# Seven small edits to a two-layer decoder trunk in fp32 on one core: unrolled MLP turns, split loads and weight tiles, an earlier spill, a changed order in the gated attention stage and at the end

## The reference, cut to what matters

```python
for layer in range(DEPTH):
    h = rmsnorm(x, norm_mix[layer])
    if layer % 2 == 0:
        m, ... = even_mixer(h, ...)   # retention and RG-LRU behind one projection
    else:
        m, gs = odd_mixer(h, ...)     # gated linear attention (GLA) by chunks
    x = x + m
    h = rmsnorm(x, norm_mlp[layer])
    x = x + jnp.square(jax.nn.relu(h @ w_up[layer])) @ w_down[layer]
y = rmsnorm(x, norm_final)
```

## Time and profile before

| | |
|---|---|
| device time, median of 3 runs | 2491.69 us (2489.11 to 2498.32) |
| the profiled execution's own time | 2490.22 us |
| its span, first to last instruction | 2488.4 us |
| TensorE (PE) matmul busy | 2436.4 us, 98% |
| DVE, ACT, POOL busy | 58%, 31%, 42% |
| mean granted TensorE clock | 0.993 of full |

### The profile page before, as it was taken

One profiled execution on the slowest core, in us unless ns is written; L12 is line 12 of the kernel. 1 busy time (PEld: TensorE's weight loads), 2 busy tenths in 40 slices (PEclk: granted clock), 3 DMA queues, 4 the chain that ended last, 5 costly groups with the idle time before them and its releaser, 6 DMA issues. The chain is left out here.

```text
span 2488.4 us, 40883 instructions
## 1 busy us (share of the span) xinstructions
PE 2436.4 (98%) x15934; PEld 2386.6 (96%) x15934; DVE 1438.0 (58%) x2082; ACT 771.0 (31%) x1222; POOL 1044.1 (42%) x773
## 2 busy tenths in 40 slices
PE   8999999999999999999999999999999999999998
PEld 8999999999999999999889889899999999999997
DVE  6974356345545544566767776756445545545576
ACT  4711442223223222223233453441222222222233
POOL 2343224354565465474212112224354554564571
PEclk9999999999999999999989999999999999999999
DMA  4123031111111111113101111131111111111112
GB/s 148 35 62 95 19 125 43 43 52 43 52 43 43 52 52 43 43 52 115 61 18 62 43 45 45 52 117 51 43 43 43 52 43 52 52 43 43 52 51 81
DMA packets 40010, 140.08 MB, mean 56 GB/s; under 512 B 6209, under 2 KB 9921, under 8 KB 38561
## 3 DMA queue, kind: packets, MB, share of 16 engines
q1 hardware_dynamic: 32192, 104.55, 13.1%
q10 hardware_dynamic: 7648, 33.04, 3.6%
HBM read 120.46 MB, written 14.88 MB: 54 GB/s over the span
## 5 line engine op out<-in xcount | busy, mean ns | idle before, releaser
L702 PE MATMUL PS<-RB,WH 128*128 128x384 f32 (+1 forms) x4368 | 1085.3, 330 | 6.3 <-issue 6.3
L702 PEld LDWEIGHTS PS<-RB,WH 128*128 128x128 f32 x4368 | 770.7, 188 | 15.5 <-issue 12.5
L702 PE MATMUL PS<-RA,WH 128*128 128x272 f32 (+2 forms) x3520 | 771.1, 309 | 11.5 <-DVE RA L1787 10.3
L702 PE MATMUL PS<-RB,WL 128*128 128x384 f32 (+1 forms) x2232 | 730.1, 327 | 0.0
L619 POOL TENSOR_TENSOR WH<-WR,FEW 128x1024 fp32r<-128x1024 f32 x128 | 247.0, 1930 | 1118.3 <-PE PS L702 1093.7
L702 PEld LDWEIGHTS PS<-RA,WH 128*128 128x128 f32 x3520 | 588.6, 188 | 16.0 <-issue 11.7
L702 PE MATMUL PS<-RA,WL 128*128 128x272 f32 (+2 forms) x1760 | 541.5, 308 | 0.0
L702 PEld LDWEIGHTS PS<-RB,WL 128*128 128x128 f32 x2232 | 420.1, 188 | 0.0
L622 POOL TENSOR_TENSOR WL<-WR,WH 128x1024 fp32r<-128x1024 f32 x128 | 340.9, 2664 | 10.0
L702 PEld LDWEIGHTS PS<-RA,WL 128*128 128x128 f32 x1760 | 331.5, 188 | 0.0
L1886 DVE TENSOR_TENSOR X<-PS,X 128x544 f32<-128x544 f32 x280 | 202.5, 724 | 203.7 <-PE PS L702 203.7
(11 more groups left out here) (223 smaller groups left out, 2335.0 us busy)
## 6 DMA issues: line engine op xcount, KB each, us to landing
WR<-ws SPq DMA_DIRECT2D x189, 512.0 KB, 3.4
X<-xT ACTq DMA_DIRECT2D x8, 544.0 KB, 7.7
EB<-xT ACTq DMA_DIRECT2D x8, 544.0 KB, 5.5
x_spill<-X ACTq DMA_DIRECT2D x1, 4352.0 KB, 15.8
EB<-x_spill ACTq DMA_DIRECT2D x8, 544.0 KB, 7.0
GA<-st_gla ACTq DMA_DIRECT2D x4, 1024.0 KB, 5.3
glas_o<-GA ACTq DMA_DIRECT2D x4, 1024.0 KB, 5.0
yT<-X SPq DMA_DIRECT2D x16, 208.0 KB, 1.9
```

The costliest lines, as they stand in the source:

```text
L702: return nc.tensor.matmul(out, lhsT, rhs, start=start, stop=stop, skip_group_check=True)
```

## The change

Seven edits. (1) Start: ACT loads tiles 0 to 3 of X and SP tiles 4 to 7; ACT and DVE split the first weight tile, and the first tile of X in three column groups; TensorE runs 16 matmuls of ONES by ONES first. (2) `parts` works in QW = 4 pieces of 256 columns; all counts of `w_high` and `w_split` are four times as large. (3) TensorE's MLP loop is written out (the other engines keep theirs). (4) The spill is 8 DMAs, one after each tile's square. (5) Even order: one half group S ahead of the first RA; RH 4 and RH 5 after RCO 3; RES earlier. (6) GLA order: L after B instead of before, GN2 after the last Q of its turn. (7) End: the last square goes to TensorE directly, `last_log` and `last_exp` are apart, and OUT_AT scales the second group later.

```diff
@@ even_schedule
-    s.append(("RA", EORDER[0]))
+    s += take(1) + [("RA", EORDER[0])]
@@
-            s += take(2 if k < 2 else 1)
+            s += take(2 if k == 1 else 1)
@@
-            s += [("RCU", 0, 0), ("RCU", 0, 1), ("RN2", 1), ("RCU", 1, 0), ("RCU", 1, 1)] + take(1) + [("RH", 4), ("RCO", 2)]
-            s += [("RCU", 2, 0), ("RCU", 2, 1), ("RX", 3, 0), ("RX", 0, 1), ("RH", 5), ("RCO", 3), ("RHL", 4)]
+            s += [("RCU", 0, 0), ("RCU", 0, 1), ("RN2", 1), ("RCU", 1, 0), ("RCU", 1, 1)] + take(1) + [("RCO", 2)]
+            s += [("RCU", 2, 0), ("RCU", 2, 1), ("RX", 3, 0), ("RX", 0, 1), ("RCO", 3), ("RH", 4), ("RH", 5), ("RHL", 4)]
@@ odd_schedule
-                if lines is not None:
-                    s.append(("L", h + 1, lines))
@@
-                if p % 3 == 1 and k > 1:
-                    s.append(("GN2",) + divmod(e - 1, 3))
                 s += ([] if norm else prep[0]) + [("B", h, c)]
...
-                s += half
+                if lines is not None:
+                    s += half[:1] + [("L", h + 1, lines)] + half[1:]
+                else:
+                    s += half
...
                 s += prep[1]
+                if p % 3 == 1 and k > 1:
+                    s.append(("GN2",) + divmod(e - 1, 3))
@@ SP
             load(0, 0)
-            sp.wait_ge(x_loaded[4], 16)
+            sp.wait_ge(x_loaded[0], 16)
+            for k in range(4, KT):
+                sp.dma_start(X[:, k, :], xT[k]).then_inc(x_loaded[k], 16)
             load(1, 1)
@@ POOL
-                nc.gpsimd.tensor_tensor(WH[:, slot, :], WR[:, slot, :], ZERO[:, 0:1].to_broadcast([P, 1024]),
-                                        ALU.add).then_inc(w_high, 1)
-                pool.wait_ge(w_high, n + 1)
-                nc.gpsimd.tensor_tensor(WL[:, slot, :], WR[:, slot, :], WH[:, slot, :].bitcast(F32),
-                                        ALU.subtract).then_inc(w_split, 1)
+                for q in range(QW):
+                    nc.gpsimd.tensor_tensor(WH[:, slot, QC * q:QC * (q + 1)], WR[:, slot, QC * q:QC * (q + 1)],
+                                            ZERO[:, 0:1].to_broadcast([P, QC]), ALU.add).then_inc(w_high, 1)
+                for q in range(QW):
+                    pool.wait_ge(w_high, QW * n + q + 1)
+                    nc.gpsimd.tensor_tensor(WL[:, slot, QC * q:QC * (q + 1)], WR[:, slot, QC * q:QC * (q + 1)],
+                                            WH[:, slot, QC * q:QC * (q + 1)].bitcast(F32), ALU.subtract).then_inc(w_split, 1)
@@ PE
-                with pe.Fori(0, MLP_TURNS) as i:
+                for i in range(MLP_TURNS):
@@
+                    nc.tensor.matmul(PS[:, 7, 0:size], ONES[:, :], RS[:, s:s + size], start=True, stop=False,
+                                     skip_group_check=True)
+                    pe.wait_ge(square_ready, 8 * 4 + KT * 3)
+                    nc.tensor.matmul(PS[:, 7, 0:size], ONES[:, :], last_square(KT - 1, size), start=False, stop=True,
+                                     skip_group_check=True).then_inc(ms_done, 1)
@@
+                        pe.wait_ge(consts_set, 1)
+                        for _ in range(16):
+                            nc.tensor.matmul(PS[:, 7, 0:P], ONES[:, :], ONES[:, :], start=True, stop=True)
                         first_step(0, RA0, 0)
@@ ACT
+                def spill(k):
+                    if layer == 0:
+                        act.dma_start(x_spill[:, k, :], X[:, k, :]).then_inc(x_spilled, 16)
@@
-                    last_squares(n0, g, range(3))
-                    last_rstd(g - 1)
+                    last_squares(n0, g, range(2))
+                    last_log(g - 1)
+                    last_squares(n0, g, range(2, 3))
+                    last_exp(g - 1)
                     last_squares(n0, g, range(3, KT))
@@
+            act.wait_ge(w_loaded[0], 16)
+            A(WH[:, 0, :], WR[:, 0, :], ACT.Copy).then_inc(w_high, QW)
             act.wait_ge(prm_loaded, 16)
+            act.wait_ge(x_loaded[0], 16)
+            for g in range(3):
+                A(RA0[:, 0, 0, grp(g)], X[:, 0, grp(g)], ACT.Copy, scale=prm(C_NORM)).then_inc(h0_high, 1)
@@
-            act.dma_start(x_spill, X[:, :, :]).then_inc(x_spilled, 16)
@@ DVE
-            OUT_AT = [(0, 0, 0, 0, 0), (0, 2, 4, 6, 8), (0, 2, 4, 5, 5)]
+            OUT_AT = [(0, 0, 0, 0, 0), (0, 2, 4, 6, 8), (0, 0, 1, 2, 3)]
@@
-                    last_add(g, KT - 1)
+                    if g < 2:
+                        last_add(g, KT - 1)
```

More of the change, by code:

```diff
@@ L168, in even_schedule @@
     assert not halves
-    s += [("RES",)] + [("RNM", 2, h) for h in range(RH)] + [("RT",)]
+    s += [("RNM", 2, h) for h in range(RH)] + [("RT",)]
     return s
@@ L737, in first_step @@
                         between()
-                    pe.wait_ge(h_low, 8 * f + at + 1)
+                    if n or at:
+                        pe.wait_ge(h_low, 8 * f + at + 1)
                     for g, (s, size) in enumerate(GROUPS):
+                        if n == 0 and at == 0:
+                            pe.wait_ge(h0_low, g + 1)
                         if at == 0 and n:
@@ L1292, in other, with high @@
                     table[0] = func
-            def high(f, k, dst, gain):
+            def high(f, k, dst, gain, counts=1):
                 scale = 1.0 if gain is None else prm(C_NORM + 8 * gain + k)
-                A(dst[:, 0, k, :], X[:, k, :], ACT.Copy, scale=scale).then_inc(h_high, 1)
+                A(dst[:, 0, k, :], X[:, k, :], ACT.Copy, scale=scale).then_inc(h_high, counts)
             def square(r, k, SQ):
@@ L1419, in mlp @@
                     square(norm, k, SQ2)
+                    spill(k)
                 for k in (4, 5):
@@ L1778, in link, with low @@
                 settle()
-            def low(f, k, dst, gain, at=None):
+            def low(f, k, dst, gain, at=None, counts=1):
                 dve.wait_ge(h_high, 8 * f + (k if at is None else at) + 1)
@@ L2015, in first_add @@
                 V.tensor_tensor(RS[:, :], RS[:, :], EB[:, 8 + k, :], ALU.add).then_inc(square_used, 1)
-            for k in range(KT):
-                low(0, k, RA0, 0)
-            dve.wait_ge(w_split, 1)
-            dve.wait_ge(w_high, 2)
-            V.tensor_tensor(WL[:, 1, :], WR[:, 1, :], WH[:, 1, :].bitcast(F32), ALU.subtract).then_inc(w_split, 1)
+            dve.wait_ge(w_high, QW)
+            V.tensor_tensor(WL[:, 0, :], WR[:, 0, :], WH[:, 0, :].bitcast(F32), ALU.subtract).then_inc(w_split, QW)
+            for g in range(3):
+                dve.wait_ge(h0_high, g + 1)
+                V.scalar_tensor_tensor(RA0[:, 1, 0, grp(g)], X[:, 0, grp(g)], prm(C_NORM), RA0[:, 0, 0, grp(g)].bitcast(F32),
+                                       ALU.mult, ALU.subtract).then_inc(h0_low, 1)
+            for k in range(1, KT):
+                low(0, k, RA0, 0, counts=2 if k == 1 else 1)
+            dve.wait_ge(w_split, QW)
+            dve.wait_ge(w_high, 2 * QW)
+            V.tensor_tensor(WL[:, 1, :], WR[:, 1, :], WH[:, 1, :].bitcast(F32), ALU.subtract).then_inc(w_split, QW)
             for k in range(1, KT):
```

72 lines of the change are left out of this document (39 added, 33 removed).

## The result

The changed kernel takes 2467.7 us (median of 6 runs, 2465.2 to 2473.2); the kernel before, in 6 runs, 2490.05. The ratio is 0.9909, 95% interval 0.9894 to 0.9925: 0.9% faster, 22 us. The forecast was 2463, with a range of 2451 to 2474. The profiled execution took 2465.2 with a span of 2463.4; against the 2488.4 of the span before that is 25.0 us, where the sum had 27.1.

The account below looks back on a forecast made before the run. With TensorE busy 98% of the span, only its standing still (about 50 us with the tail) and its half-speed clock could be shortened. The terms summed to 27.1 us off the profiled 2490.2, so 2463 us, range 2451 to 2474.

Parts of the forecast that it names:

- Start: Start of the kernel: TensorE begins at 7.5 at full speed and ends step 0 4.3 us earlier, 0.2 given back; 4.1 us.
- Turns written out: Both MLPs: TensorE's four waits at two back jumps each, with no releaser, go; 6.3 us, ends 5 and 6.3.
- Weight tiles in four pieces: GLA: shorter POOL instructions let DVE in between, so TensorE waits less; 5 of 13.5 us back, ends -3 and 10.
- Rival A: GLA: the lock between DVE and POOL is only cut up, DVE's total delay stays; sum 17.7, time 2472.5; chance 0.25.
- Order of GLA: GLA: state's product ahead of the logits' reading in bank 7, 2.1 us; GN2 out of the way of X and Q, 1.
- L1687: TensorE's wait of 1.0 us at this source line goes with POOL's pieces; 1 us.
- Spill by tile: Spill of X: DVE no longer waits for the one DMA of X, as eight issues end before GLA; 1.6 us.
- Even order: Even stage: half group ahead of first RA hides 0.7, RES earlier, most else taken back; together 1.9 us, ends 0.7 and 4.
- End: Kernel's end: DVE adds the last product sooner, no longer held up by scaled outputs; 2.2 us, ends 1 and 2.7.
- Clock: GLA: half speed cost 6.8 us after waits of over 2 us; with these shorter, half returns: 3.4 us.
- D: Rival: slower, POOL becomes the bound and TensorE waits for weights above 1.47 us an instruction; about 2523; chance 0.02.
- B: Rival: all clears, GLA waits go from 18 to 3 us and the clock holds; 36 us in sum, 2454; chance 0.15.

## Why the prediction was right, and where it was wrong

The time lay in the range and the direction was right; the forecast's 27.1 us stands against 25.0 in the traces and 22.3 between the medians. Step by step:

- **Start** (4.1, measured 2.8). The start of step 1 came 3.9 us earlier (forecast 4.3). The step that failed is "0.2 is given back": by the lead it was 1.1. DVE's sums were put from 19.3 to 29.0; they ran from 20.4 to 30.1, since they follow ACT's squares, which start only at 18.3, behind the last tiles of X and the second weight tile. Taking the products of ONES away changed the lead by 0.1, as that wait covers them.
- **Turns written out** (6.3, measured 7.4 by the lead, 7 to 9.5 by the run). Right. The idle rows left out about 1 us. The Trainium skill (Runtime: NRT & Kernel Launch, "Instruction fetch mechanics") says that a taken branch to a target outside the window of prefetched instructions has to fetch before it goes on. No run here shows the fetch; that the written out code has none of the four stops agrees with it.
- **Weight tiles in four pieces** (5, measured 16 to 19). The mechanism was right in kind and the size was off: 7 to 10 us less waiting, and 6 to 7 us less lost to the clock. The forecast took a share of the waits of rows 2 as they stood, but with the new order of L they would have been larger, and it booked the clock separately. What the pieces are worth with both L and GN2 in their old places was not run. Rival A rested on a total that stays; DVE's busy time fell by 99 us over the program. The rule of the Trainium skill (SBUF — State Buffer, "Who interferes with whom"), that one excludes the other for a whole instruction, is not at odds with that. What was wrong was to conclude that cutting leaves the sum of the blocks as it is. Why the sum falls is not shown here.
- **Order of GLA** (L 2.1, measured a loss of 8 to 9; GN2 1, measured 14 to 15 beside that L, 2 to 4 without it). This is the step that failed with its sign: "the state's product standing behind the reading of the logits in bank 7; now it stands in front. 2.1 us". Whoever stands behind waits, and the new one behind is the logits matmul. The rows of the order in the section on the change show it directly behind the 128x256 product, with no half step between: `half` is empty in that turn and in its like in head 2, where the two longest waits are. In the other four turns of the kind one half step stands between. The old order had a half step and B's four 128x128 products between L and the state's product, so the new distance is shorter even there, and DVE comes to the state later: around 1394 us its reading ends 3.0 us behind the product, where in the same turn before the reading of the logits ended 2.2 us behind them. Two of these four turns wait 1.05 us each. The 1.5 set against new waits was no estimate of this one, which could have been priced: DVE's list between the two readings was there to be counted.
- **L1687** (1). The wait is gone in the changed kernel and with two pieces, and back with one piece (1.0 us, at L1190), so it went with the pieces as forecast.
- **Spill by tile** (1.6, measured 4 to 6). Right in kind. The measured wait is 2.9, the clock behind it adds 1.7, and the landing time of one DMA of 4.4 MB differs by 1.2 us between two runs.
- **Even order** (1.9). The lead grows by 1.6 over the stage, of which 0.9 (the wait of 0.7 at 217 us) is shown to be the order's. The rest lies within what differs from run to run. That DVE's chain sets the end of the stage, as the forecast said, is borne out.
- **End** (2.2, measured 3.0). Right in sum, though the step named as the cause, the outputs that held up DVE's add, gives only 1.0 of it.
- **Clock** (3.4, measured 0). "With these shorter, I take half": the waits that went were in part replaced, and the lost clock was the same, 17 us at half speed in GLA in both traces. With L back and GN2 back, where the waits in GLA are many and short, the granted clock is 0.996 in the mean of four runs, against 0.993 before. So the term was there to be had, though not with this order.

So the near hit is partly luck: the pieces brought some 11 us more than their term, the order of L came out 10 us below its own, and the clock brought nothing. Nor do the parts add up: undone one at a time, the pieces, GN2, the turns and the spill less L make some 37 us, against the 22 that all of it brought, since GN2's place costs so much only beside the new place of L, and the later of two waits can hide the earlier, as with the products of ONES. Of the rivals, D (POOL the bound) can be left out: TensorE never waits for a weight tile, and POOL's instructions take 0.79 and 0.91 us where D needed more than 1.47. A named waits in GLA of over 12 us as its sign, and they were 11.9, but they were new ones and not the old ones moved. B (all clears, 36 us) is what the kernel with L back comes near, with 30 to 31.

**A version that beats both.** The changed kernel with L in its old place: 2458.8 us, 0.9876, 30 to 31 us below the kernel before. Neither the kernel with GN2 back as well nor the one with the logits a turn later can be told from it.

## What to carry to other kernels

When a bank or buffer has two users and one waits for the other's reader, swapping them is no gain in itself: look at what then stands between the new pair on the matrix engine, and count what the reading engine does first. Put enough other work between, and check by the times of both engines that it is enough: here one half step of 2.1 us was not in two turns. Undo edits in pairs as well as one at a time: here GN2's place cost 14 us beside one place of L and 2 to 4 beside the other. And where a lowered clock follows waits, a wait's price can be more than its own length; measure it by times of several runs, not by one trace.

## What the runs showed of the hardware that was not expected

- POOL in shorter pieces makes DVE faster in sum, not only sooner: the same 2084 instructions are busy 1438.2 us beside POOL's tiles in one piece, 1383.2 in two and 1339.1 in four, while POOL goes from 1040.4 over 1147.7 to 1278.7.
- The granted clock of one kernel differs from run to run. One kernel (L back, one piece) had granted clocks from 0.988 to 0.995 and times from 2479.5 to 2465.3 us in four runs on one chip, with the same order of instructions (only the fastest was profiled). In all twelve kernels of the experiments the clock in the mean of the runs lay between 0.9909 and 0.996, the lowest in the two kernels with the most waiting in GLA (one piece with L after B; GN2 back with L after B), the highest with L and GN2 both back. What makes it fall in one run and not in the next is not settled by these runs.
- Half speed at the start cost nothing in the end: without the products of ONES TensorE's matmuls took 0.52 instead of 0.34 us until 12.7 us, and the lead from 60 us on was 2.7 instead of 2.8.
